# New order of joins and convolution, and the gated pairs' block sums on GpSimd, in a hybrid encoder kernel

## The reference

```
def conv_ffn(hn, w_ffn_in, conv_w, conv_b, w_ffn_down):
    u, v = jnp.split(hn @ w_ffn_in, 2, axis=-1)          # 2816 columns each
    pad = CONV_W // 2
    up = jnp.pad(u, ((0, 0), (pad, pad), (0, 0)))
    L = u.shape[1]
    uc = conv_b
    for t in range(CONV_W):
        uc = uc + up[:, t:t + L] * conv_w[t]
    return (jax.nn.gelu(uc) * v).astype(dt) @ w_ffn_down
```

## Time and profile before

| | |
|---|---|
| median of 3 runs (lowest to highest) | 1283.27 us (1282.43 to 1284.66) |
| the profiled execution | 1282.7 us, its span 1280.9 us |
| PE, PEld, DVE busy in the span | 95%, 87%, 68% |
| ACT, POOL busy in the span | 41%, 15% |
| mean granted clock of PE | 0.986 |

### The profile page before, as it was taken

The page is one execution under the profiler, slowest core; times in us unless marked ns, Lnnn a source line. Parts: engine busy times, 40 slices in busy tenths (PEclk is TensorE's granted clock), DMA queues, the critical chain, the costliest instruction groups (busy, mean ns, idle before and its releaser), DMA issues.

```text
span 1280.9 us, 18435 instructions
## 1 busy us (share of the span) xinstructions
PE 1219.8 (95%) x6989; PEld 1108.8 (87%) x6989; DVE 875.3 (68%) x1189; ACT 528.7 (41%) x832; POOL 195.6 (15%) x137
## 2 busy tenths in 40 slices
PE   6999999999999999999999979899899899899977
PEld 5999999999999988888888869789789789789965
DVE  7494585486377372232233799988998998898987
ACT  5353353335245152122221456535535535535544
POOL 0000000000000000000000314324324333433340
PEclk9999999999999999999999999999899899899989
DMA  4311111101201011111123012112121121121302
GB/s 168 134 35 49 68 44 50 61 33 49 78 33 49 34 54 62 66 62 69 65 94 131 22 66 80 53 68 81 50 77 72 50 83 66 50 82 67 115 17 99
DMA packets 23185, 86.14 MB, mean 67 GB/s; under 512 B 2512, under 2 KB 2768, under 8 KB 23120
## 3 DMA queue, kind: packets, MB, share of 16 engines
q1 hardware_dynamic: 22544, 83.90, 17.7%
q10 hardware_dynamic: 576, 1.38, 0.3%
HBM read 82.12 MB, written 3.15 MB: 67 GB/s over the span
## 4 chain that ended last, share of the span: by engine, by line
PE 83%; DVE 10%; issue 2%; DVEq 2%; ACT 1%; DMA 1%; POOL 0%; SPq 0%; ACTq 0%; POOLq 0%
PE ps L1507 43%; PE ps L1750 19%; PE ps L1833 10%; PE ps L1604 3%; PE ps L1544 3%; DVE ring L1232 2%; PE ps L1597 1%; PE ps L1614 1%; PE ps L1532 1%; DVE cb L1315 1%; DVE cb L1296 1%; DVEq L1301 1%; DVE af L1251 1%; PE ps L1534 1%; DVE h L1219 1%
## 5 line engine op out<-in xcount | busy, mean ns | idle before, releaser
L1507 PE MATMUL ps<-hn,ring 128*128 128x256 f32 (+1 forms) x2544 | 462.6, 337 | 0.3 <-DVE hn L921 0.3
L1507 PEld LDWEIGHTS ps<-hn,ring 128*128 128x128 f32 x2544 | 388.3, 191 | 46.7 <-issue 0.7
L1750 PE MATMUL ps<-af,ring 128*128 128x384 f32 x1848 | 334.0, 340 | 33.0 <-DVE v L1288 21.0
L1750 PEld LDWEIGHTS ps<-af,ring 128*128 128x128 f32 x1848 | 325.8, 191 | 40.3 <-DVE v L1288 22.3
L1833 PE MATMUL ps<-ring,gf 128*128 128x512 f32 x693 | 161.0, 394 | 7.1 <-DVE gf L1331 6.8
L892 DVE TENSOR_TENSOR ring<-raw,ring 128x1024 fp32r<-128x1024 f32 x68 | 83.1, 1224 | 119.2 <-ACT ring L476 114.8
L1833 PEld LDWEIGHTS ps<-ring,gf 128*128 128x128 f32 x693 | 132.0, 191 | 35.1 <-issue 7.8
L1232 DVE TENSOR_TENSOR ring<-raw,ring 128x512 fp32r<-128x512 f32 x164 | 127.5, 810 | 13.5 <-ACT ring L713 13.3
L713 ACT ACTIVATE ring<-raw 128x512 fp32r<-128x512 f32 x164 | 96.6, 621 | 53.2 <-DMA raw<-in_pairs 42.0
L1467 POOL TENSOR_TENSOR sums<-raw 128x512 f32<-128x512 f32 x1 | 1.3, 1283 | 707.0 <-DMA raw<-in_pairs 707.0
L525 ACT ACTIVATE sig<-ps 128x768 f32<-128x768 f32 x36 | 29.2, 812 | 179.9 <-PE ps L1507 179.9
(11 more groups left out here) (171 smaller groups left out, 1297.8 us busy)
## 6 DMA issues: line engine op xcount, KB each, us to landing
raw<-in_units SPq DMA_DIRECT2D x68, 512.0 KB, 3.4
raw<-in_pairs SPq DMA_DIRECT2D x66, 512.0 KB, 3.5
strips<-in_strips SPq DMA_DIRECT2D x4, 896.0 KB, 4.6
x_in<-in_x_s SPq DMA_DIRECT2D x4, 512.0 KB, 5.4
h<-in_x_s SPq DMA_DIRECT2D x1, 2048.0 KB, 8.0
y_s<-hw SPq DMA_DIRECT2D x4, 512.0 KB, 3.0
x_in<-in_x_p SPq DMA_DIRECT2D x2, 512.0 KB, 7.4
h<-in_x_p SPq DMA_DIRECT2D x1, 1024.0 KB, 10.4
```

What stands on the lines that cost most here:

```text
L1507: ins = pe.matmul(out, w if stationary_w else x, x if stationary_w else w, start=start and i == 0, stop=stop and i == 2)
L1750: ins = pe.matmul(ps[:, bank, 0:HALF], ring[:, p, a, k * P:(k + 1) * P], af[:, x, b, k, :], start=first and k == 0 and j == 0, stop=k == H ...
```

## The change

It has three parts.

1. In the up turns, `conv(i-1)` moves on DVE from behind `join_last(i-1)` to ahead of `join_first(i)`. At the end of a stage, `conv` and `join_last` of the last pair move behind the first piece steps of the down projection, `join_last` behind `conv`; `gate` and `gate_lo` of this pair, and `gelu` and `gate_hi` on ACT, move one step back too.
2. The four block sums leave `gate` on DVE. GpSimd makes them in a new `gate_sums`, called in its list of weight differences behind S3 of the next pair, or at a stage's end behind S2 of the last down pair (`SUMS_AT`). It waits for the gated product.
3. In the last stage, `gate_hi(20)` goes ahead of `gelu(21)` on ACT and `gate_lo(20)` ahead of `conv(21)` on DVE; before, `gate_lo(20)` stood among the block sums.

PE and SP have the same instructions in the same order.

```diff
+SUMS_AT = {}
+for _lo, _hi, _qs in STAGES:
+    for _i in range(_lo + 1, _hi):
+        if _i % 2 == 0:
+            SUMS_AT[(_i + 1, S3) if _i + 1 < _hi else (down_pair(_qs[-1]), S2)] = _i - 1
+SUMS_AT[down_pair(LAST_Q), S2] = NF - 1
...
-                gelu(hi - 1)
                 if hi == NF:
                     gate_hi(NF - 2)
+                    gelu(hi - 1)
                     gate_hi(NF - 1)
                 for n, x in enumerate(DOWN[d]):
                     hi_upto(PLACE[down_pair(qs[-1]), x] + 6)
-                    if n == 1 and hi < NF:
+                    if n == 0 and hi < NF:
+                        gelu(hi - 1)
+                    if n == 2 and hi < NF:
                         gate_hi(hi - 1)
...
                 dve.tensor_tensor(cb[:], cb[:], v2[:], ALU.mult).then_inc(g32_done, 1)
-                dve.tensor_tensor(GATE[S3], ge[:, 0:HALF], ge[:, HALF:T], ALU.subtract).then_inc(gs_done, 1)
-                dve.wait_ge(g32_done, i + 1)
-                dve.wait_ge(gs_done, 4 * q + 1)
-                dve.tensor_tensor(GATE[S2], GATE[A22], GATE[S3], ALU.subtract).then_inc(gs_done, 1)
-                dve.tensor_tensor(GATE[S1], ge[:, HALF:T], GATE[A22], ALU.add).then_inc(gs_done, 1)
-                if i == NF - 1:
-                    gate_lo(i - 1)
-                dve.wait_ge(gs_done, 4 * q + 2)
-                dve.wait_ge(g_lo, gate_form(q, A11))
-                dve.tensor_tensor(GATE[S4], GATE[A12], GATE[S2], ALU.subtract).then_inc(gs_done, 1)
...
                     lo_upto(PLACE[i, A12] + 5)
+                    if i > lo:
+                        conv(i - 1)
                     if i > 0:
                         join_first(i)
                     if i > lo:
                         lo_upto(PLACE[i - 1, S4] + 5)
                         join_last(i - 1)
-                        conv(i - 1)
...
-                join_last(hi - 1)
-                conv(hi - 1)
                 if hi == NF:
+                    join_last(hi - 1)
+                    gate_lo(NF - 2)
+                    conv(hi - 1)
                     gate(NF - 1)
-                    gate_lo(NF - 1)
+                    gate_lo(NF - 1, GATES[1:3])
+                    gate_lo(NF - 1, GATES[3:])
...
                     if hi < NF:
+                        if n == 0:
+                            conv(hi - 1)
+                            join_last(hi - 1)
                         down_sums(d, hi, qs, x, range(3))
-                        if n == 0:
+                        if n == 1:
                             gate(hi - 1)
-                        elif n == 1:
+                        elif n == 2:
                             gate_lo(hi - 1)
...
+            def gate_sums(i):
+
+                q = i // 2
+                pool.wait_ge(g32_done, i + 1)
+                pool.tensor_tensor(GATE[S3], ge[:, 0:HALF], ge[:, HALF:T], ALU.subtract).then_inc(gs_done, 1)
+                pool.wait_ge(gs_done, 4 * q + 1)
+                pool.tensor_tensor(GATE[S2], GATE[A22], GATE[S3], ALU.subtract).then_inc(gs_done, 1)
+                pool.tensor_tensor(GATE[S1], ge[:, HALF:T], GATE[A22], ALU.add).then_inc(gs_done, 1)
+                pool.wait_ge(gs_done, 4 * q + 2)
+                pool.wait_ge(g_lo, gate_form(q, A11))
+                pool.tensor_tensor(GATE[S4], GATE[A12], GATE[S2], ALU.subtract).then_inc(gs_done, 1)
+
             pool.wait_ge(t_done, DIFF[1, S3])
             for j, x in DIFFS[7:]:
                 difference(pool, j, x)
+                if (j, x) in SUMS_AT:
+                    gate_sums(SUMS_AT[j, x])
```

More of the change, by code:

```diff
@@ L1315, in gate, with gate_lo @@
                 dve.tensor_tensor(cb[:], cb[:], v2[:], ALU.mult).then_inc(g32_done, 1)
-                dve.tensor_tensor(GATE[S3], ge[:, 0:HALF], ge[:, HALF:T], ALU.subtract).then_inc(gs_done, 1)
-                dve.wait_ge(g32_done, i + 1)
-                dve.wait_ge(gs_done, 4 * q + 1)
-                dve.tensor_tensor(GATE[S2], GATE[A22], GATE[S3], ALU.subtract).then_inc(gs_done, 1)
-                dve.tensor_tensor(GATE[S1], ge[:, HALF:T], GATE[A22], ALU.add).then_inc(gs_done, 1)
-                if i == NF - 1:
-                    gate_lo(i - 1)
-                dve.wait_ge(gs_done, 4 * q + 2)
-                dve.wait_ge(g_lo, gate_form(q, A11))
-                dve.tensor_tensor(GATE[S4], GATE[A12], GATE[S2], ALU.subtract).then_inc(gs_done, 1)
-            def gate_lo(i):
+            def gate_lo(i, forms=None):
                 q = i // 2
-                for x in GATES[:1] if i % 2 == 0 else GATES[1:]:
+                for x in forms or (GATES[:1] if i % 2 == 0 else GATES[1:]):
                     dve.wait_ge(g_hi, gate_form(q, x))
```

## The result

| | before | after |
|---|---|---|
| median (lowest to highest) | 1283.19 us (1282.43 to 1284.66) | 1333.28 us (1333.07 to 1336.13) |
| span of the profiled execution | 1280.9 us | 1331.4 us |
| granted clock of PE | 0.986 | 0.971 |

The changed kernel takes 1.0394 times as long (95% interval 1.0376 to 1.0412), 50.1 us more. The forecast was 1321 us in 1292 to 1345: the sign and the range held, the point was 12 us low.

The account below looks back on a forecast made before the run. PE, busy nearly all of the 1280.9 us span, was taken as the bound. 1280.9 + 40.9 + 3.2 + 0 - 6 = 1319.0 us of span, so 1321 us, range 1292 to 1345.

Parts of the forecast that it names:

- gaps in the turns: Up turns: S1 waits for the longer chain of centre, conv and joins; 40.9 us in all, between 7.9 and 57.
- slow matmuls: Behind the gaps of turns 1 and 3: PE's clock is halved, 2 x 1.6 = 3.2 us.
- gaps at the four stage ends: Stage ends: what join_third frees is waited off at S2, behind the first tile sums; 0 us, -10 to +14.
- last stage: Last stage: PE's 6.8 us gap for gate_lo(20) goes, then S2 waits for tile sums; gain 6 us (2 to 8).
- worse: Turns and stage ends: six long gaps halve the clock (+6.4), sums hold gate_lo longer (+13.6); 1341 us, chance 0.17.
- signs that were named: Turns: PE waits for join_last, 1 to 6 us; conv above 6 us; no join_third wait; h wait at third down form.
- their bound: Turns 1, 3, 7, 11, 15, 19: slow matmuls behind all six long gaps, 0 to 9.6 us.
- the step on what is late next: Last stage: once the gate_lo(20) gap goes, S2 waits for the first tile sums, done at 1235 against PE at 1241.

Follow-up runs that it names:

- part 2 alone: The kernel before with only the four block sums moved to GpSimd, the order on DVE as before: 1300.74 us, 1.014.
- part 3 alone: The kernel before with only gate_hi(20) ahead of gelu(21) and gate_lo(20) ahead of conv(21): 1282.26 us, 0.9989.
- GpSimd kept quiet: The kernel before with only the turns' new order, and GpSimd's first difference of the next pair made to wait for conv: 1304.51 us, 1.0175.

## Why the prediction was right, and where it was short

The forecast was a span longer by 38.1 us; it was 50.5. Term by term:

| term | forecast | measured |
|---|---|---|
| gaps in the turns | 40.9 | 33.6 |
| slow matmuls | 3.2 | 16.3 |
| gaps at the four stage ends | 0 | +1.5 |
| last stage | -6 | -1.5 |

The measured terms are PE's idle time, and for the slow matmuls its busy time. The errors are -7.3, +13.1, +1.5 and +4.5 us, so the first hides part of the others, and that the point came within 12 us is in part luck. 1333.28 us lies just above the forecast's own 1308 to 1333, in the stretch given to the rival "worse". Half of that rival happened, slow matmuls behind all six long gaps of the turns; its other half, the sums holding `gate_lo` 3.4 us longer at each stage end, did not.

- **The turns.** Right in kind and place. PE's new gaps are 4.3 us in turns 7, 11, 15 and 19 (forecast 4.8), 1.1 us in turns 6, 10, 14, 18, 20 and 1.4 in turn 2 (1.6), 1.35 us in turn 21 (1.7), and 4.5 and 3.9 us more in turns 1 and 3 (5.2 each). Turn 7 of after:

```profile
906.38 0.71 ACT L787 ACTIVATE cb<-u,vecs 128x384 f32<-128x384 f32 x1
907.12 5.26 DVE L1306 SCALAR_TENSOR_TENSOR cb<-u,vecs,cb 128x511 f32<-128x511 f32 x4
907.30 1.72 POOL L335 TENSOR_TENSOR raw<-raw 128x512 f32<-128x512 f32 x1 [3.80 <-DVE ring L1242]
909.10 1.34 POOL L340 TENSOR_TENSOR tb<-raw 128x512 f32<-128x512 f32 x1
910.39 1.71 POOL L343 TENSOR_TENSOR raw<-raw 128x512 f32<-128x512 f32 x1
```

The chain from the end of `centre(6)` (907.1) to that of `join_last(6)` (913.9) is 6.8 us, forecast 7.8: all three differences did fall into it, but `conv` took 5.26 and not 6.25. Three of its operations were held (1.51, 1.60 and 1.48 us), and the first was not (0.75), since it had begun 0.18 us before the first difference. S1(7) was due 2.6 us behind `centre`, forecast 3.0. The 6.25 came from a misread row: the working took the 6.34 us of the earlier trace rows for `conv` beside three differences, and a fourth lay beside its first operation:

```profile
1220.32 1.29 POOL L332 TENSOR_TENSOR tb<-raw 128x512 f32<-128x512 f32 x1
```

So 6.34 us is the time beside four, and each costs some 1.0 us and not 1.3. The signs that were named are there, except that `conv` stays below 6 us everywhere and that PE's whole gap in turn 1 is 6.6 us, 2.1 of which stood before. One bound was too low: without GpSimd in the chain the forecast had 0.9 us in turn 7. The run that kept it off `conv` has 2.36: 0.8 more for the held piece, and 0.5 more since S1(7) was due 2.5 us behind `centre` and not 3.0.

- **The clock is the term that was mis-sized**, 16.3 us for 3.2. Two steps failed. The larger is in the turns: the forecast priced the slow matmuls only behind the two longest gaps and put the four of turns 7 to 19 at nothing, though their bound went to 9.6 for six gaps. In after, each of the six is followed by 1.1 to 2.5 us of extra matmul time (108 took 19.3 us in before, 84 take 14.9), and of the 17.9 us in the two groups 13.0 stand in the turns. The other is at the stage ends, 4.6 us, where the forecast compared only when S2 starts. S2 starts 19.1 us behind the end of the last S3 (20.3 before), but in before the slow matmuls were those ahead of S2 and are in its start time; now the gap is next to S2 and the slow ones come behind it. The run with part 2 alone shows this by itself: S2 0.2 us later, and 1.8 to 2.2 us more in the 90 matmuls behind than the 20.7 that they take without a long gap.

- **The stage ends.** The gap of `join_third` did go and did come back at S2, four times 5.28 us for 5.25. The 0.34 us for a piece ahead of it was not foreseen. With the slow matmuls the four stage ends cost 6.0 us, where the forecast booked 0.

- **The last stage.** Here the step on what is late next failed. It said the tile sums; after, as with part 3 alone, it is a weight piece of A12, behind `gate_lo(21)` on DVE:

```profile
1271.51 10.40 PE L1853 MATMUL ps<-ring,gf 128*128 128x512 f32 x45
1287.23 29.19 PE L1853 MATMUL ps<-ring,gf 128*128 128x512 f32 x117 [5.32 <-DVE ring L1242]
```

The Trainium skill (GPSIMD Engine Reference, 1. Specifications) names the shared SBUF interfaces as the cause of such contention; the rows agree for `conv`, which took 2.37 us with GpSimd made to wait and 5.28 without that wait. Of the 28.7 us, keeping it off `conv` gave back 6.6 to 7.4.

## What to carry to other kernels

An operation moved ahead of the one that another engine waits for costs, at each wait, its length less the room that the trace shows there; here PE came to wait in 13 turns, and keeping the other engine off the moved operation gave back only a quarter of the loss. When a wait is freed, look for the next one on the same chain, and count slow matmuls behind the place where the gap will be, not where it was. What helped was to put the operations that nobody waits for soon (`join_last`, `conv`, pieces that are five products ahead) behind the tile sums that PE waits for.

## What the runs showed of the hardware

- **The clock after a gap.** In the feed-forward parts of the runs above, a gap of 1.7 us or less had no slow matmuls behind it, one of 3.8 us or more always had them, 1.1 to 2.9 us more than the same matmuls take without a long gap (12 up matmuls in 2.35 us, 84 in 14.9, 108 in 19.3, 90 of the down projection in 20.7). Between these it varies from place to place and with equal gaps. Two gaps of the kernel with GpSimd kept quiet, 2.36 and 2.34 us long, with 108 matmuls behind each:

```profile
904.02 20.58 PE L1753 MATMUL ps<-af,ring 128*128 128x384 f32 x108 [2.36 <-DVE v L1282]
1101.22 19.00 PE L1753 MATMUL ps<-af,ring 128*128 128x384 f32 x108 [2.34 <-DVE v L1282]
```
```profile
904.02:910.02 6.00, 6.00 (x25) 6.00 (x26) 4.33 (x4) 2.27 (x4) 3.60 (x3) 0.72 0.51 175
1101.22:1107.22 6.00, 6.00 (x34) 6.00 (x35) 5.27 (x6) 3.70 (x7) 3.62 (x3) 1.00 0.54 176
```

The granted clock of the first 6 us is 0.72 in one and 1.00 in the other. The Trainium skill (TensorE: Matmul & The Clock Gate, Part 1) says that the default state is the lower clock and that recent activity releases it, at a moment that varies between equal runs; these two gaps agree with that, and the price of a gap is here a range and not a number.

- **Small gaps.** Splitting 5.3 us of waiting at a stage end into 1.7, 0.7 and 1.7 us gave back 1.2 us of waiting and 1.5 to 2.3 us of matmul time (90 matmuls in 20.9 us, against 22.4 to 23.3 in the run with the sums behind `join_third`).

- **DVE with an operand in PSUM.** `join_last` took 0.54 us, all of it beside a GpSimd difference (903.03 to 904.63), and the piece just ahead of it, with both inputs in SBUF, 1.51 in place of 0.7 (above, turn 7 of the kernel with GpSimd kept quiet).
